# Two transformer blocks on one core: routing rebuilt, level scores in half-width products, and matmuls moved into waits

## The chip, the cores and the metric

The kernel runs on one NeuronCore of a Trainium2 chip. The metric is device time in microseconds, the median of several executions. The engines named here are TensorE (PE, with its weight load PEld), VectorE (DVE), ScalarE (ACT), GpSimd (POOL) and SyncE (SP), whose queue starts most of the DMAs.

## The reference

x is 256 tokens by 1024, f32. Two blocks run one after the other. Shortened to what matters here:

```
# block one
h = rmsnorm(x);  parts = h @ w_in
o_a = gated delta rule(short conv + silu of q, k, v)        # rope positions serve branch b
o_b = attention over 64 keys that an indexer chose (top-k)
x = x + (sigmoid(gate_a)*(o_a @ w_proj_a) + sigmoid(gate_b)*(o_b @ w_proj_b)) @ w_out
# experts: top 1 of 4 groups, then top 2 of the 4 experts in it
gsel = argmax(glog);  top_p, top_i = top_k(softmax(elog[gsel]), 2)
wts = softmax(glog)[gsel] * top_p / sum(top_p)
x = x + sum_e wts_e * (silu(xt @ w1_e) * (xt @ w3_e)) @ w2_e;   x = rmsnorm(x)
# block two
branch a: scores[t,s] = sum_c q[t,c] k[s,c] exp(b[t,c] - b[s,c]), s <= t, then state; branch b: attention
x = x + (gates and branches) @ w_out_2;   x = x + ffn(x);   x = x + sigmoid(.. @ w_ple_gate) * (p @ w_ple_proj)
```

The activations are f32. Weights and activations of the large products are split into a rounded part (fp32r) and the remainder, and each product is three matmuls: high by high, low by high, high by low.

## The kernel before

**Weights.** About 148 chunks of up to 128 x 2048 words come in one fixed order through a ring of four raw buffers (SP, L478). ScalarE rounds a chunk into `w_hi` (`ahead`, L566) and VectorE subtracts it into `w_lo` (`ahead`, L1838); each of these two has three buffers. `ahead(i)` splits all chunks up to i + 2. A raw buffer is loaded again when its low part is made, so the split of one chunk releases the load of the fourth after it. Every engine's program is written out by hand, in one order, with semaphores between them; an engine does not pass a wait, so all that is queued behind it waits too.

**Block one up to its routing.** TensorE makes the convolution's channels, turns them (`turn_y`, L1225) and makes the token blocks in between. ScalarE takes the turned tiles out of PSUM (L700); ahead of that stands the sine for the rope (L692), for which VectorE reduces the angles (down to L1965). Gate chunks 0 to 7 fill TensorE's time beside the delta rule and the top-k; ScalarE takes each out with a sigmoid (`gate_sigmoid`, L686). Chunk 7 goes to bank 7 as one, and the first projection, into banks 6 and 7, waits for both of its sigmoids. Then come `turn_probs` (L1480), `prob_times_v` (L1491) and projections (`project`, L1056 to L1059). `prob_times_v` waits until ScalarE has the turned probabilities in SBUF (L817); its outputs are 64 columns wide in the array, one half for even heads and one for odd. VectorE has the softmax and its multiplication (L2204) in its order between weight splits.

**Routing.** After the last half of x is ready, ScalarE sums squares, TensorE turns x and multiplies by the router (L1522). VectorE picks the group (`one_hot`), with L1879 in the root before it. TensorE sums the ranks of the tokens in their groups (`ranks`, L1555 to L1559, f32), among them the group counts, last. VectorE orders the groups by count (L2389 on), writes `order_i` (L2395), by which SP knows whose expert weights to load, and then the one-hot matrix `place` of token by slot (L2405). `gather` (L1564) multiplies x by `place` in f32 for each of the eight column groups; ScalarE and VectorE split each result (`gathered_high`, `gathered_low`). Between these VectorE works out the expert weights of each token and puts them into `scal` (`s_comb`); `slot_tiles` (L1584, L1589) multiplies them to slots and turns `place`. Expert 0's gate comes as two half chunks (`FIRST`, `FIRST + 1`), then `slot_tiles`, then the up chunk (`FIRST + 2`, L1542 to L1544). All 16 experts follow.

**Level scores of block two.** The scores of branch a are made level by level: for level n a pair of operands is multiplied, 8 tiles of 128 x 128 (L1711), and VectorE takes the masked places into `hsc` (`copy_predicated`, L2483). Level 0 takes the diagonal, levels 1 to 6 places inside the two 64 x 64 diagonal blocks, level 7 the block between the halves. Between levels stands one weight chunk (`LVL2[n]`, L1111 to L1113).

**End of attention in block two.** Gate chunks 6 and 7, `turn_probs`, `prob_times_v`, then projections; ScalarE evicts gate 7 ahead of the turned probabilities. GpSimd multiplies each gate chunk by a row of roots (L546).

## Time and profile before

| | |
|---|---|
| median of 3 runs | 903.81 us (903.46 to 904.65) |
| profiled execution: time / span | 902.36 us / 900.6 us |
| busy: PE, PEld, DVE, ACT, POOL | 97%, 90%, 69%, 54%, 5% of the span |
| mean granted TensorE clock | 0.994 of full |
| DMA | 156.73 MB, mean 174 GB/s |
| TensorE busy in the stretch 260 to 280 us | 14.56 of 20 us |
| TensorE busy in the stretch 500 to 560 us | 60 of 60 us |

A row of the timeline has start, duration, engine, line, operation, tiles and the number of instructions merged, and in brackets how long the engine was idle before it and what ended that. A matmul's duration includes its way through the array, so in a stream the starts, not the durations, tell the rate. One f32 product is two passes, and each stands in the trace as an instruction. `128*64` is 128 rows by 64 columns of the array in use.

### The profile page before, as it was taken

Reading aid. Unit: us, or ns where it says so; the run is one execution under the profiler, and the core shown is the slowest. Engines: PE = TensorE matmul, PEld = TensorE weight load, DVE = VectorE, ACT = ScalarE, POOL = GpSimd, SP = SyncE. Lnnn points to the kernel's source line nnn. Section 1 sums busy time; section 2 is a strip of 40 time slices with the busy share of each in tenths; the row PEclk is TensorE's granted clock in tenths of the full one; section 3 lists DMA queues with packets and bytes.
Section 4 is the critical chain, followed back from the end, with each engine's and each line's share of the span. In section 5 each row is a group of like instructions: output and inputs, shape, how many; then the busy total and the mean of one; then the engine's idle time right before and its main releaser. Section 6 shows DMA issues by size and latency. Waiting matters only on the chain.

```text
span 900.6 us, 16480 instructions
## 1 busy us (share of the span) xinstructions
PE 873.4 (97%) x7186; PEld 809.4 (90%) x7186; DVE 622.4 (69%) x761; ACT 484.6 (54%) x580; POOL 43.2 (5%) x66
## 2 busy tenths in 40 slices
PE   8999999998998999999999999999999999999997
PEld 8988899998977999999979888998989999999986
DVE  6879477698847964568887887886565655555564
ACT  5647713657525754367766643767545443343463
POOL 6000060000000000000000000121000000000000
PEclk9999999999998999999999999999999999999999
DMA  8846310424107985569975444253355656556421
GB/s 248 292 148 212 94 51 3 141 95 141 47 1 252 363 302 206 186 237 360 359 229 192 165 141 140 95 194 128 101 188 176 209 190 199 173 186 199 176 94 47
DMA packets 88904, 156.73 MB, mean 174 GB/s; under 512 B 7432, under 2 KB 61184, under 8 KB 84864
## 3 DMA queue, kind: packets, MB, share of 16 engines
q1 hardware_dynamic: 88144, 154.90, 50.9%
q8 instruction: 56, 0.92, 0.4%
q10 hardware_dynamic: 688, 0.79, 0.3%
q14 instruction: 16, 0.13, 0.0%
HBM read 154.62 MB, written 1.05 MB: 173 GB/s over the span
## 4 chain that ended last, share of the span: by engine, by line
PE 77%; DVE 14%; ACT 4%; SPq 2%; issue 2%; DMA 1%; POOL 0%; DVEq 0%; POOLq 0%; ACTq 0%
PE ps L1056 9%; PE ps L1059 8%; PE ps L1058 8%; PE ps L1111 7%; PE ps L1112 7%; PE ps L1113 7%; DVE w_lo L1838 5%; PE ps L1542 4%; PE ps L1543 4%; PE ps L1544 4%; PE ps L1310 3%; PE ps L1614 2%; PE ps L1616 2%; PE ps L1615 2%; ACT w_hi L566 2%
## 5 line engine op out<-in xcount | busy, mean ns | idle before, releaser
L1838 DVE TENSOR_TENSOR w_lo<-raw,w_hi 128x2048 fp32r<-128x2048 f32 (+2 forms) x148 | 334.1, 2263 | 136.7 <-ACT w_hi L566 135.4
L566 ACT ACTIVATE w_hi<-raw 128x2048 fp32r<-128x2048 f32 (+2 forms) x148 | 277.8, 1881 | 81.4 <-PE ps L1113 27.4
L1056 PE MATMUL ps<-h_hi,w_hi 128*128 128x256 f32 x736 | 210.5, 286 | 2.2 <-DVE h_lo L1848 1.4
L1058 PE MATMUL ps<-h_lo,w_hi 128*128 128x256 f32 x736 | 208.2, 283 | 0.0
L1059 PE MATMUL ps<-h_hi,w_lo 128*128 128x256 f32 x736 | 208.2, 283 | 0.0
L1056 PEld LDWEIGHTS ps<-h_hi,w_hi 128*128 128x128 f32 x736 | 141.1, 192 | 4.8 <-issue 3.2
L1058 PEld LDWEIGHTS ps<-h_lo,w_hi 128*128 128x128 f32 x736 | 141.1, 192 | 0.4
L1059 PEld LDWEIGHTS ps<-h_hi,w_lo 128*128 128x128 f32 x736 | 141.1, 192 | 0.0
L1111 PE MATMUL ps<-w_hi,h_hi 128*128 128x512 f32 (+1 forms) x240 | 93.9, 391 | 0.5 <-DVE h_lo L2247 0.5
L1112 PE MATMUL ps<-w_lo,h_hi 128*128 128x512 f32 (+1 forms) x240 | 92.7, 386 | 0.0
L1113 PE MATMUL ps<-w_hi,h_lo 128*128 128x512 f32 (+1 forms) x240 | 92.6, 386 | 0.0
L1542 PE MATMUL ps<-w_hi,arena_rounded 128*128 128x256 f32 x320 | 91.1, 285 | 0.7 <-DVE w_lo L1838 0.6
L1544 PE MATMUL ps<-w_hi,arena_rounded 128*128 128x256 f32 x320 | 89.4, 280 | 0.0
L1543 PE MATMUL ps<-w_lo,arena_rounded 128*128 128x256 f32 x320 | 89.4, 279 | 0.0
L1542 PEld LDWEIGHTS ps<-w_hi,arena_rounded 128*128 128x128 f32 x320 | 60.0, 188 | 1.9 <-DVE w_lo L1838 1.1
L1543 PEld LDWEIGHTS ps<-w_lo,arena_rounded 128*128 128x128 f32 x320 | 60.2, 188 | 0.5
L1544 PEld LDWEIGHTS ps<-w_hi,arena_rounded 128*128 128x128 f32 x320 | 60.0, 188 | 0.0
L1111 PEld LDWEIGHTS ps<-w_hi,h_hi 128*128 128x128 f32 x240 | 45.1, 188 | 8.7 <-DVE h_lo L2247 0.7
L1113 PEld LDWEIGHTS ps<-w_hi,h_lo 128*128 128x128 f32 x240 | 45.1, 188 | 8.4
L1112 PEld LDWEIGHTS ps<-w_lo,h_hi 128*128 128x128 f32 x240 | 45.2, 188 | 7.9
L1056 PE MATMUL ps<-o_hi,w_hi 128*128 128x256 f32 x128 | 36.6, 286 | 2.0 <-DVE w_lo L1838 1.0
L1111 PE MATMUL ps<-w_hi,o_hi 128*128 128x512 f32 x96 | 37.8, 394 | 0.3 <-DVE o_lo L2285 0.3
(456 smaller groups left out, 1352.1 us busy)
## 6 DMA issues: line engine op xcount, KB each, us to landing
raw<-in_w_in SPq DMA_DIRECT2D x35, 1024.0 KB, 5.3
raw<-in_w_exp_up SPq DMA_DIRECT2D x16, 1024.0 KB, 6.0
raw<-in_w_exp_down SPq DMA_DIRECT2D x16, 1024.0 KB, 5.7
raw<-in_w_exp_gate SPq DMA_DIRECT2D x15, 1024.0 KB, 5.8
raw<-in_w_ffn_gate SPq DMA_DIRECT2D x11, 1024.0 KB, 5.4
raw<-in_w_ffn_up SPq DMA_DIRECT2D x11, 1024.0 KB, 5.4
raw<-in_w_ffn_down SPq DMA_DIRECT2D x11, 1024.0 KB, 4.9
raw<-in_w_out SPq DMA_DIRECT2D x8, 1024.0 KB, 5.1
```

What stands on the lines that cost most here:

```text
L566: act.activation(w_hi[:, j % SPL, 0:kt * n], raw[:, j % RAW, 0:kt * n], ACT.Copy).then_inc(w_high, 1)
L1056: pe.matmul(o, hi[:, k, cols], a_hi[:, k, :], start=(k == 0 and (whole or c == 0)), stop=False)
L1058: pe.matmul(o, hi[:, k, cols], a_lo[:, k, :], start=False, stop=False)
L1059: last_mm = pe.matmul(o, lo[:, k, cols], a_hi[:, k, :], start=False, stop=(k == kt - 1 and (whole or c == len(outs) - 1)))
L1111: pe.matmul(o, a_hi[:, k, tok], hi[:, k, cols], start=(first and k == 0), stop=False)
L1112: pe.matmul(o, a_hi[:, k, tok], lo[:, k, cols], start=False, stop=False)
L1113: last_mm = pe.matmul(o, a_lo[:, k, tok], hi[:, k, cols], start=False, stop=(end and k == kt - 1))
L1310: m = pe.matmul(by_head(o, rows_c, h), left[rows_c, t, h, :], right(rows_c, h), start=True, stop=True)
L1542: pe.matmul(o, xs_hi[:, k, slots], hi[:, w_k, :], start=(k == 0), stop=False)
L1543: pe.matmul(o, xs_hi[:, k, slots], lo[:, w_k, :], start=False, stop=False)
L1544: last_mm = pe.matmul(o, xs_lo[:, k, slots], hi[:, w_k, :], start=False, stop=(k == KD - 1))
L1838: dve.tensor_tensor(w_lo[:, j % SPL, 0:kt * n], raw[:, j % RAW, 0:kt * n], w_hi[:, j % SPL, 0:kt * n].bitcast(F32), sub).then_inc(w_ready, 1)
```

## The change

- `w_in` part: the sine (L692) goes behind the six evictions of turned tiles; the semaphores of positions and p are joined with others.
- The last gate chunk of block one is made tile by tile, the first into bank 7, the second into bank 6, each with its own sigmoid; the first projection begins with the two tiles of bank 7.
- A third tile of projection (0, 1, 0) goes ahead of `prob_times_v`; in block two half of gate chunk 7 goes behind `turn_probs`, and its eviction behind `prob_tiles`.
- Level scores: levels 0 to 6 multiply only the two 64 x 64 diagonal blocks, level 7 only the block between.
- Routing: the choice of group is written in bf16 too, the counts are multiplied first and signalled by themselves, in bf16. Expert choice moves behind the slots, the gathered low parts and the splits of the first three expert chunks, and is worked out by comparisons of all pairs. x is rounded into `x_hi` by ScalarE behind its squares and `x_lo` is subtracted by GpSimd; the gather is four fp32r products for each column group. GpSimd also makes `tok_pos`. TensorE turns the identity 10 times ahead of the ranks and 24 times behind them.

```diff
@@ scalar, block one
-            ahead(TOK[0][0])
-            act.wait_ge(s_trig, 1)
-            act.activation(cs[:, :, :, :], cs[:, :, :, :], ACT.Sin).then_inc(s_sin, 1)
...
                 act.activation(qkv[:, t, 512 * g:512 * g + 512], bank(j % 4), ACT.Copy).then_inc(s_qkv, 1)
+            act.wait_ge(s_trig, 1)
+            act.activation(cs[:, :, :, :], cs[:, :, :, :], ACT.Sin).then_inc(s_sin, 1)
...
-            gate_sigmoid(7)
+            last_gate_sigmoid()
@@ scalar, in front of the routing
                 squares(1, c)
+                cols = slice(512 * c, 512 * c + 512)
+                act.activation(x_hi[:, :, cols], x_tok[:, :, cols], ACT.Copy).then_inc(s_x_hi, 1)
@@ scalar, routing()
-                for k in range(4):
+                for k in range(6):
                     gathered_high(k)
                 ahead(FIRST + 1 - SPL)
-                for k in range(4, 6):
-                    gathered_high(k)
-                ahead(FIRST + 2 - SPL)
@@ gpsimd
+            for c in range(2):
+                pool.wait_ge(s_x_hi, c + 1)
+                cols = slice(512 * c, 512 * c + 512)
+                pool.tensor_tensor(x_lo[:, :, cols], x_tok[:, :, cols], x_hi[:, :, cols].bitcast(F32),
+                                   ALU.subtract).then_inc(s_x_lo, 1)
+            pool.wait_ge(s_place, 1)
+            step(pool.tensor_tensor(ttmp_p, ga1.unsqueeze(2)..., sel16.unsqueeze(1)..., ALU.mult))
+            for j in range(1, 4):
+                step(pool.tensor_tensor(tok_pos, ttmp_p[:, :, :, 0] if j == 1 else tok_pos, ttmp_p[:, :, :, j], ALU.add))
+            pool.tensor_copy(scal[:, :, 16], r_moe).then_inc(s_comb, 1)
@@ tensor, last gate and projections of block one
-            gate_chunk(GATE, 7, s_gate_ev)
+            for c in range(2):                  # tile 0 to bank 7, tile 1 to bank 6 behind gate 6's eviction
+                if c == 1:
+                    pe.wait_ge(s_gate_ev, 7)
...
+                m.then_inc((s_last_gate, w_used)[c], 1)
+            pe.wait_ge(s_last_gate, 2)
+            project(PROJ, 0, 0, 0, (2, 3), False)
             pe.wait_ge(s_gate_ev, 8)
-            project(PROJ, 0, 0, 0)
+            project(PROJ, 0, 0, 0, (0, 1), True)
...
             turn_probs(prob, 0, range(2, 6))
+            project(PROJ, 0, 1, 0, (2,))
             prob_times_v(prob_t, ..., 0)
-            project(PROJ, 0, 1, 0, range(2, 4))
+            project(PROJ, 0, 1, 0, (3,))
@@ tensor, ranks(), gather(k), routing()
+                pe.matmul(bank(3)[:, 8:12], ones_bf[:, :], g[:, 0, :], start=True, stop=False)
+                pe.matmul(bank(3)[:, 8:12], ones_bf[:, :], g[:, 1, :], start=False, stop=True).then_inc(s_small_ps, 1)
+                pe.matmul(o[:, 0:4], upto_bf[:, :], g[:, 0, :], start=True, stop=True)
...
-                for t in range(NT):
-                    m = pe.matmul(bank((4 + k) % 8)[:, 0:S], by_row(x_tok)[:, t, k, :], place[:, t, :],
-                                  start=(t == 0), stop=(t == NT - 1))
+                for part in (x_hi, x_lo):
+                    for t in range(NT):
+                        m = pe.matmul(bank((4 + k) % 8)[:, 0:S], by_row(part)[:, t, k, :], place_r[:, t, :], ...)
...
+                idle_turns(10)
                 ranks()
+                idle_turns(24)
                 pe.wait_ge(s_place, 1)
+                pe.wait_ge(s_x_hi, 2)
+                pe.wait_ge(s_x_lo, 2)
@@ tensor, level scores
+                blocks = ((0, 0), (1, 1)) if n < len(LEVELS) else ((0, 1),)
                 for u in range(8):
                     b = bank(2 * (n % 2) + u // 4)[:, P * (u % 4):P * (u % 4) + P]
                     left, right = (hk[:, u, :], hq[:, u, :]) if n == 0 else (hx[:, n % 2, u, :],) * 2
-                    m = pe.matmul(b, left, right, start=True, stop=True)
+                    for keys, queries in blocks:
+                        r, c = slice(64 * keys, 64 * keys + 64), slice(64 * queries, 64 * queries + 64)
+                        m = pe.matmul(b[r, c], left[:, r], right[:, c], start=True, stop=True)
@@ tensor, block two
-            gate_chunk(GATE2, 7, s_gate_ev2)
+            gate_chunk(GATE2, 7, s_gate_ev2, range(4))
             turn_probs(prob2, 2)
+            gate_chunk(GATE2, 7, s_gate_ev2, range(4, 8))
@@ vector, routing
-            one_hot(ga1, gl, gs1)
-            dve.nop().then_inc(s_group, 1)
+            is_top(ga1, gl, gs1)
+            dve.tensor_tensor(group_bf[:, :, :], ga1, last(gs2, 4), ALU.is_equal).then_inc(s_group, 1)
+            step(dve.tensor_tensor(ga1, ga1, last(gs2, 4), ALU.is_equal))
...
+            step(dve.memset(lower, 0.0))        # with the other constants, ahead of the merge of block one
+            for i in range(1, 4):
+                m = mark(dve.memset(lower[:, i, 0:i], 1.0))
+            dve.wait_ge(s_dve, m)
...
             m.then_inc(s_place, 1)
+            ...                                 # the group's expert logits and both shifts, 5 instructions
+            for k in range(4):
+                gathered_low(k)
+            ahead(FIRST + 1 - SPL)
+            for k in range(4, 8):
+                gathered_low(k)
+            ahead(FIRST + 2 - SPL)
+            ahead(FIRST + 3 - SPL)
             dve.wait_ge(s_rle, 2)
             step(dve.tensor_reduce(gs3, gl, X, add_))
+            step(dve.tensor_tensor(ttmp, by_j, by_i, ALU.is_equal))
+            step(dve.tensor_tensor(ttmp, ttmp, lower..., mult))
+            step(dve.tensor_tensor(above, by_j, by_i, ALU.is_gt))
+            step(dve.tensor_tensor(ttmp, ttmp, above, add_))
+            step(dve.tensor_reduce(e1h, ttmp, X, add_))
+            step(dve.scalar_tensor_tensor(e1h, e1h, 1.5, el, ALU.is_lt, mult))
+            ...                                 # sum, factors, reciprocal: 5 instructions
+            dve.wait_ge(s_comb, 1)
             dve.tensor_tensor(scal[:, :, 0:16]..., last(tok_pos, 4), e1h..., mult).then_inc(s_comb, 1)
```

## Rows read from the trace of the kernel before

**Rows 1.** The page: the chain that ended last, and a group of instructions.

```profile
PE 77%; DVE 14%; ACT 4%; SPq 2%; issue 2%; DMA 1%; POOL 0%; DVEq 0%; POOLq 0%; ACTq 0%
...
L566 ACT ACTIVATE w_hi<-raw 128x2048 fp32r<-128x2048 f32 (+2 forms) x148 | 277.8, 1881 | 81.4 <-PE ps L1113 27.4
```

**Rows 2.** Waits, whole span: total us, times, longest.

```profile
ACT cs L692 <- DVE cs L1965: 4.7, 1, 4.7
...
DVE arena L2483 <- PE ps L1711: 10.1, 7, 2.4
...
PE ps L1491 <- ACT arena L817: 1.9, 2, 1.0
PE ps L1225 <- ACT arena L700: 1.6, 1, 1.6
```

**Rows 3.** Timeline of TensorE, 205 to 216 us: start, duration, instructions.

```profile
207.11 0.39 PE L1056 MATMUL ps<-o_hi,w_hi 128*128 128x256 f32 x1 [0.93 <-ACT arena L686]
...
213.41 1.06 PE L1480 MATMUL ps<-ident,arena 128*128 128x128 f32 x8 [0.28 <-DVE arena L2204]
```

**Rows 4.** Timeline of TensorE around narrow products and one level.

```profile
512.60 1.95 PE L1711 MATMUL ps<-arena 128*128 128x128 f32 x16
514.30 0.48 PE L1111 MATMUL ps<-w_hi,h_hi 128*128 128x512 f32 x1
...
156.38 0.68 PE L1381 MATMUL ps<-arena 64*64 64x64 f32 x16
156.89 1.09 PE L1391 MATMUL ps<-arena 64*64 64x64 f32 x16
...
221.41 3.11 PE L1491 MATMUL ps<-arena 128*64 128x128 f32 x48 [0.84 <-ACT arena L817]
```

**Rows 5.** Timeline of TensorE in the routing.

```profile
269.10 0.59 PE L1555 MATMUL ps<-small,upto 128*128 128x4 f32 x2 [1.59 <-DVEq L2380]
...
274.83 9.36 PE L1564 MATMUL ps<-arena,x_tok 128*128 128x256 f32 x32 [3.43 <-DVE arena L2405]
...
287.43 1.06 PE L1584 MATMUL ps<-small,arena 128*128 128x17 f32 x8
...
289.62 0.39 PE L1542 MATMUL ps<-w_hi,arena_rounded 128*128 128x256 f32 x1 [0.65 <-DVE w_lo L1838]
```

**Rows 6.** Windows: busy of PE, PEld, DVE, ACT, POOL; granted clock; DMA.

```profile
268.00:269.00 1.00, 0.00 (x0) 0.00 (x0) 0.82 (x5) 0.00 (x0) 0.00 (x0) 0.50 0.00 0
277.00:278.00 1.00, 1.00 (x3) 0.73 (x3) 0.45 (x2) 0.44 (x1) 0.00 (x0) 0.50 1.03 381
278.00:279.00 1.00, 1.00 (x6) 1.00 (x5) 0.11 (x2) 0.47 (x1) 0.00 (x0) 0.92 1.00 385
```

**Rows 7.** Timeline of VectorE in the routing.

```profile
266.19 0.17 DVE L1879 TENSOR_SCALAR small<-small 128x2 f32<-128x2 f32 x1
...
271.43 0.16 DVE L2389 SCALAR_TENSOR_TENSOR small<-ps,small 128x4 f32<-128x4 f32 x1 [1.40 <-PE ps L1559]
...
272.67 0.17 DVE L2395 CAST order_i<-small 128x4 int32<-128x4 f32 x1
```

**Rows 8.** DMA issues from 274.8 us: count, KB, median us to landing.

```profile
raw<-in_w_exp_up SPq DMA_DIRECT2D x1, 1024.0 KB, 7.8
```

**Rows 9.** GpSimd's line L546: duration ns min/median/max.

```profile
L546 POOL TENSOR_TENSOR arena<-arena x8: 1270/1864/2119, 576.4 to 625.3; 128x512 f32<-128x512 f32 x8
```

**Rows 10.** Timeline of all engines, 576 to 578.5 us.

```profile
576.36 1.95 POOL L546 TENSOR_TENSOR arena<-arena 128x512 f32<-128x512 f32 x1 [445.21 <-ACT arena L674]
...
577.47 0.87 DVE L2524 TENSOR_SCALAR small<-small 128x16 f32<-128x16 f32 x1
```

**Rows 11.** Timeline of SyncE's queue and of VectorE's split of that chunk.

```profile
274.81 0.37 SPq L478 DMA_DIRECT2D raw<-in_w_exp_up  x1
...
287.28 2.29 DVE L1838 TENSOR_TENSOR w_lo<-raw,w_hi 128x2048 fp32r<-128x2048 f32 x1
```

More of the change, by code:

```diff
@@ L262, in two_block_program @@
         act_s2, act_p2 = (view(4096 + 1024 * n, 2, NT, D_EXP) for n in range(2))
-        place = view(6144, NT, S)
+        place_r = view(6144, NT, S, of=arena_rounded)
+        place = place_r.bitcast(F32)
+        x_hi, x_lo = (view(12288 + 2048 * n, NT, DM, of=arena_rounded) for n in range(2))
         x_cols = view(18448, KD, S)
@@ L322, in two_block_program @@
         top8b = small[:, 464:472]
+        lower = split3(small[:, 536:552], 4)
+        above, ttmp_p = (split4(small[:, first:first + 32], 2, 4) for first in (552, 584))
         glog_twice = split3(small[:, 536:616], 2)
@@ L2363, in _, with is_top @@
             root_of(1, r_moe)
-            def one_hot(dst, src, top):
+            def is_top(dst, src, top):
                 step(dve.tensor_reduce(top, src, X, ALU.max))
@@ L2370, in one_hot @@
                 step(dve.tensor_reduce(gs2, dst, X, ALU.max))
-                step(dve.tensor_tensor(dst, dst, last(gs2, 4), ALU.is_equal))
             dve.wait_ge(s_small_ps, 1)
@@ L2404, in _ @@
             for t in range(NT):
-                m = dve.tensor_scalar(place[:, t, :], count, slot2[:, t:t + 1], None, ALU.is_equal)
+                m = dve.tensor_scalar(place_r[:, t, :], count, slot2[:, t:t + 1], None, ALU.is_equal)
             m.then_inc(s_place, 1)
+            step(dve.tensor_tensor(ttmp, rl[:, :, 4:20].rearrange("p t (g j) -> p t g j", j=4), last(ga1, 4), mult))
+            step(dve.tensor_reduce(el, ttmp.rearrange("p t g j -> p t j g"), X, add_))
+            dve.tensor_tensor(gl, gl, last(gs1, 4), sub).then_inc(s_rlm, 1)
@@ L2408, in _ @@
+            step(dve.tensor_reduce(gs3, el, X, ALU.max))
+            dve.tensor_tensor(el, el, last(gs3, 4), sub).then_inc(s_rlm, 1)
+            for k in range(4):
[5 more added lines that the diff above has]
+            ahead(FIRST + 3 - SPL)
             dve.wait_ge(s_rle, 2)
             step(dve.tensor_reduce(gs3, gl, X, add_))
-            step(dve.reciprocal(gs3, gs3))
```

95 lines of the change are left out of this document (47 added, 48 removed).

## The prediction

> **What bounds the kernel now.** I read the page's chain first: 77% of it is TensorE's own work and 14% VectorE's [rows 1]. So a microsecond is won only where TensorE works less, or where it stands waiting. The list of waits then shows where it stands: 1.6 us at the turn of the convolution tiles (L1225), 1.9 us in two waits ahead of probabilities times values (L1491), and the routing [rows 2, 5]. There TensorE starts the ranks at 269.10, the gather at 274.83, the slot tiles at 287.43 and the first up chunk at 289.62. The windows show its clock at 0.50 from 268 on, and back during 278 to 279: it fell after small router matmuls and half a microsecond of waiting, and rose 3.4 us into the gather [rows 6]. The level stage of the second block has no TensorE wait; VectorE waits for it 10.1 us in 7 times [rows 2]. All times are those of the profiled execution.
>
> **The change part by part.**
>
> *Sine behind the evictions.* ScalarE stood 4.7 us in front of the sine (L692), and everything behind it was late, up to the eviction that TensorE waited 1.6 us for at L1225 [rows 2]. With the sine moved behind the six evictions that wait goes: TensorE reaches the turn 1.6 us earlier, ScalarE is by then through. The sine's result is wanted far later. **-1.6 us** (bounds 0 and -1.7).
>
> *Last gate chunk in two tiles.* It removes the 0.93 us before L1056 at 207.11. But the next thing TensorE needs is the probabilities: it waits for VectorE's L2204 at 213.41, and VectorE has come there from the top-k without a pause [rows 3]. The stall only moves there: **0** (bounds 0 and -0.9).
>
> *Project tile ahead of probabilities times values; last half gate chunk likewise in block two.* Each fills a wait of about 0.95 us at L1491 [rows 2] with 12 or 24 matmuls that stood behind it. In the first block VectorE's path to the merge starts earlier by it, but gets four memsets with two semaphore waits in front of it, about 0.2 us. **-0.7 and -1.0 us** (bounds 0 and -1.9 together). The later eviction of gate 7 in block two stays covered: its sigmoid comes after the projections.
>
> *The level scores.* Today 8 levels have 16 passes of 128x128 each, started at 512.60, and the next weights follow at 514.30: 1.70 us a level [rows 4]. After, seven levels have 32 passes of 128 rows by 64 columns, with 64 moving columns, alternating between the two column halves; the eighth has 16, all in one half. No row has this form. The nearest: L1381 alternates between column halves in the same 64 rows and takes 156.89 - 156.38 = 0.51 us for 16 passes, 32 ns each; L1491 alternates over all 128 rows with 128 moving columns, 48 passes in 3.1 us, 64 ns each, where a full-width pass of the same length takes 106 ns. So halves do run side by side. L1391, all in one corner, starts 16 passes within 1.09 us less the 0.22 us of its last: 58 ns each [rows 4]. At 29 to 32 ns a level costs 0.93 to 1.0 us, and the eighth 16 x 0.058 = 0.93. Entering and leaving the narrow form costs about 0.1 us each: L1491 ends 3.11 us after its start, though 48 x 0.055 would be 2.6. I take 1.13 us a level, so 8 x (1.70 - 1.13) = **-4.6 us**; without the switches -6.2, with 0.3 us of them -3.8; and, if halves took turns, 7 x (1.86 + 0.2 - 1.70) - 0.6 = +1.9. VectorE has 10.1 / 7 = 1.4 us to spare in a level [rows 2], so it does not become the bound at 0.6 us less.
>
> The Trainium skill (TensorEngine Tiling (Array Packing), Key Properties) says that a change of tiling mode drains the engine, here twice a level. It gives no price; taken as nothing the levels give -6.2 us, with the row's 0.2 us -4.6.
>
> *Routing, the head.* Group counts come first, in bf16. VectorE stood 1.40 us before L2389 at 271.43, for ranks that began at 269.10 at half clock [rows 5, 7]. Two short products in place of ten passes should let it begin 1.75 us earlier. Against that, the low part of x is now subtracted by GpSimd. Its 512 elements take at least 1.27 us [rows 9], so 1024 take 2.5, from about 266.25 (behind the last squares) to 268.8. In the trace L2524, 16 elements, takes 0.87 us and ends at 578.34, when GpSimd's instruction begun at 576.36 ends, at 578.31 [rows 10]; L1879, 2 elements, takes 0.17 [rows 7]. So VectorE's small operations are held by one of GpSimd. The group choice would be held about 0.5 us. I take the order of groups 1.3 us earlier (bounds 0.2 and 1.75), so ready at 272.84 - 1.3 = 271.5, and with it the expert weights' issue.
>
> *Routing, the tail.* Here the expert choice stands behind three chunk splits on VectorE, and the third chunk (first up) has to land. It was issued at 274.81 [rows 11] and landed 7.8 us later, at 282.6 [rows 8], so 9.8 us after the order at 272.84 [rows 7]. The sum after: 271.5 + 9.8 = 281.3 landed; ScalarE's half of the split 1.9 [rows 1] and VectorE's 2.2 [rows 11] with two handovers of 0.1 gives 285.6; then 13 small operations, at the 0.207 us that the six from 271.43 to 272.67 took each, 2.7, gives 288.3; TensorE's slot tiles begin at 288.4 instead of 287.43. They take 1.5 us (289.62 - 287.43 less the 0.65 of waiting), and the up chunk begins at 289.9 against 289.62: **+0.3 us** (bounds -0.2 and +2.5). The gather itself, 9.36 us now [rows 5], is in one pass per product and wholly hidden in this, as long as it ends some 3 us before 281; if it did not, its lateness would be added.
>
> *The clock in the tail.* From the end of the new gather (about 277.5) to 288.4 TensorE has two short half chunks of gate, 1.4 us each, and waits in between, the last one from 283.9 on, 4.5 us; no identity turns are put there. Before, the clock fell after less waiting than that [rows 6]. If it falls, slot tiles and the first up matmuls run at half rate. Before, it rose 3.4 us after steady work began; between once and twice that at half rate costs 1.7 to 3.4 us; I take **+2.4**. Before, this stretch ran at full rate, the low stretch lay under the waits and the gather. What the turns of the identity in the head win, an earlier rise, is spent under the wait for the up chunk.
>
> Sum of the likeliest: -1.6 - 0.7 - 1.0 - 4.6 + 0.3 + 2.4 = -5.2 us, on the profiled execution 902.36 - 5.2 = 897.2. The median of the runs is 1.45 above the profiled one: 903.81 - 5.2 = **898.6**.
>
> **The rivals.**
> - *The clock holds in the tail* (or its loss lies under waits). For: two bursts of work stand in it. Against: 4.5 us of waiting at its end. -7.6 us: 896.2.
> - *GpSimd's subtraction holds VectorE.* It begins within 0.1 us of L1879 at 266.19 [rows 7], a small operation in front of the root. If L1879 comes second it waits until 268.8 and all of the head with it; the order then comes 2 us later than taken. -3.2 us: 900.6. The Trainium skill (SBUF — State Buffer, Who interferes with whom) has this as a lock: a VectorE instruction with two SBUF inputs, or in a two-port mode, and a GpSimd instruction that reads SBUF exclude each other for the whole instruction, and whoever starts first has it; L2524 agrees.
> - *The column halves take turns* (slower side). If a pass with all 128 rows occupied goes one after the other at 58 ns, the levels cost +1.9 instead of -4.6. Against: L1491 and L1381. It decides from about 54 ns a pass on, where seven levels no longer win. The rest is -0.6, so +1.3 us: 905.1.
> - *The filled waits come back.* The wins of L1225 and L1491 are taken by VectorE chains behind them as that of the last gate is. -2.0 us: 901.8.
>
> **How the numbers follow.** Chances: forecast 0.50, clock holds 0.20, GpSimd 0.12, halves take turns 0.10, waits come back 0.08. A measurement of this kernel tells 0.2% (1.8 us) from no change. Faster by more: the first three whole and half of the last, 0.86; within: 0.06; slower by more: 0.08, of the case of turns with its upper bounds. Low end: switches at nothing and the clock holding, -10, 894. High end: GpSimd's hold with a low clock's upper bound, 902.5; nearly all of the turns case is left out.
>
> **What would show it.** L1711 at 29 to 32 ns a pass and 1.1 us a level, VectorE's wait there down from 1.4 to about 0.8 us; no wait at L1225; at L1491 under 0.2 us. The order of groups 1.3 us earlier against the squares, and still the first up chunk not earlier, with TensorE waiting some 4 us before the slot tiles for VectorE's expert choice; the granted clock at 0.50 there. The prediction is wrong if the up chunk lands or the choice is through much sooner, if L1711 passes take over 50 ns, or if the clock stays full.

## The result and the profile after

The changed kernel took 899.1 us (median of 5 runs, 897.85 to 900.15) against 903.81: a ratio of 0.9947, 95% interval 0.9932 to 0.9961. The forecast was 898.6. The profiled execution took 898.25 us, its span 896.5, with a mean granted clock of 0.993; 897.2 was forecast for it.

I set the start of each TensorE instruction beside the start of the same one before. "Shift" below is start after less start before, and the times in the table are those of the kernel before. The difference of two shifts is what the stretch between them won (negative) or lost.

| stretch (shift at its end) | forecast | between the traces |
|---|---|---|
| sine (-1.53 at 128 us) | -1.6 | -1.5 |
| last gate chunk and project tile, block one (-2.13 at 239 us) | 0, -0.7 | -0.6 |
| routing up to the first up matmul (+0.90) | +0.3 | +3.0 |
| low clock behind it (+2.37 at 292 us) | +2.4 | +1.5 |
| experts (+1.01 at 454 us) | 0 | -1.4 |
| eight level scores (-2.95 at 558 us) | -4.6 | -4.0 |
| last half gate chunk, block two (-4.05 at 628 us) | -1.0 | -1.1 |
| sum | -5.2 | -4.1 |

The total came out close to the forecast partly by luck. The routing cost 2.7 us more than forecast and the level scores won 0.6 less; the experts won 1.4 us that was not forecast, and the low clock cost 0.9 less than taken. What is left between the two traces is 1.1 us.

The page of the kernel after, the chain that ended last (to [rows 1]):

```profile
PE 84%; DVE 9%; ACT 2%; SPq 2%; issue 1%; DMA 1%; POOL 0%; DVEq 0%; POOLq 0%
```

TensorE's own work is 84% of the chain now (77% before) and VectorE's 9% (14%).

The waits of the kernel after, whole span (to [rows 2]):

```profile
PE ps L1636 <- DVE small L2490: 3.4, 1, 3.4
...
DVE arena L2537 <- PE ps L1766: 3.2, 3, 1.9
...
PE ps L1521 <- DVE arena L2259: 1.4, 1, 1.4
```

The waits at the turn of the convolution tiles and ahead of probabilities times values are gone. New is the first row: TensorE stands 3.4 us before the slot tiles for the last product of the expert choice. VectorE's waits for the level scores fell from 10.1 us in seven to 3.2 in three. Not all of that is gone: between 500 and 560 us VectorE now waits 2.9 us for ScalarE's rounded chunks (0.9 before). The last row is the wait that the last gate chunk was forecast to hand on: 0.28 us before [rows 3], 1.44 now.

Timeline of TensorE around one level (to [rows 4]):

```profile
519.67 0.39 PE L1142 MATMUL ps<-w_hi,h_lo 128*128 128x512 f32 x1
519.99 1.15 PE L1766 MATMUL ps<-arena 128*64 128x64 f32 x32
521.07 0.50 PE L1140 MATMUL ps<-w_hi,h_hi 128*128 128x512 f32 x1
```

From the first pass to the next weights it is 1.08 us instead of 1.70, with 29 ns from pass to pass on the average (two passes start 7 ns apart, and 58 ns lie between one pair and the next). But the first pass starts 0.32 us behind the last weight pass, and in the kernel before it was 0.23: the period of a level went from 7.24 to 6.75 us, 0.49 less and not 0.57.

Timeline of the routing, of all engines (to [rows 5, 7, 11]):

```profile
264.03 2.34 POOL L555 TENSOR_TENSOR arena_rounded<-x_tok,arena_rounded 128x1024 fp32r<-128x1024 f32 x1 [3.94 <-ACT arena_rounded L953]
264.05 2.35 DVE L1935 TENSOR_SCALAR small<-small 128x2 f32<-128x2 f32 x1
...
270.49 0.17 DVE L2449 CAST order_i<-small 128x4 int32<-128x4 f32 x1
...
272.64 7.98 PE L1612 MATMUL ps<-arena_rounded 128*128 128x256 f32 x32
...
279.12 1.05 ACT L589 ACTIVATE w_hi<-raw 128x1024 fp32r<-128x1024 f32 x1
...
282.91 3.42 DVE L1894 TENSOR_TENSOR w_lo<-raw,w_hi 128x1024 fp32r<-128x1024 f32 x2
...
286.24 0.15 DVE L2476 TENSOR_REDUCE small<-small 128x2 f32<-128x8 f32 x1
...
289.22 1.07 PE L1636 MATMUL ps<-small,arena_rounded 128*128 128x17 f32 x8 [3.37 <-DVE small L2490]
...
290.52 0.36 PE L1584 MATMUL ps<-w_hi,arena_rounded 128*128 128x256 f32 x1
```

Three things are to be seen. VectorE's tensor_scalar of two elements takes 2.35 us beside GpSimd's subtraction, and both end together. The gather takes 8 us. And the choice (L2476 on) begins when VectorE has split the up chunk, which began late: the first expert chunk landed at 275.69, and ScalarE came to it at 279.12, behind six gathered parts.

Windows of the kernel after (to [rows 6]); the third number from the end is the granted clock:

```profile
263.00:264.00 1.00, 0.59 (x4) 0.60 (x4) 1.00 (x3) 0.95 (x2) 0.00 (x0) 0.78 0.00 0
264.00:265.00 1.00, 1.00 (x6) 1.00 (x7) 0.96 (x2) 0.00 (x0) 0.97 (x1) 0.50 0.00 0
...
270.00:271.00 1.00, 1.00 (x9) 1.00 (x8) 0.83 (x7) 0.00 (x0) 0.00 (x0) 0.81 0.00 0
...
290.00:291.00 1.00, 1.00 (x10) 1.00 (x10) 0.65 (x2) 0.14 (x1) 0.00 (x0) 0.93 1.00 418
291.00:292.00 1.00, 1.00 (x7) 1.00 (x6) 1.00 (x1) 0.98 (x2) 0.00 (x0) 0.50 0.18 74
```

The clock falls in the router now, behind a wait of 0.42 us, some 4 us earlier than before, and again behind the slot tiles. That second low stretch was forecast, the first was not.

### The profile page after: what moved, and what is told of

The parts are those of the page before. It is cut to its first block, busy times and chain, and to the rows that moved or that the text cites. A ratio compares the mean times of both kernels' runs of the same rounds, so it can differ in the third digit from the quotient of the medians.

```text
span 896.5 us, 16763 instructions
## 1 busy us (share of the span) xinstructions
PE 873.4 (97%) x7327; PEld 808.8 (90%) x7327; DVE 623.3 (70%) x755; ACT 486.5 (54%) x582; POOL 51.6 (6%) x75
## 3 DMA queue, kind: packets, MB, share of 16 engines
HBM read 154.62 MB, written 1.05 MB: 174 GB/s over the span
## 4 chain that ended last, share of the span: by engine, by line
PE 84%; DVE 9%; ACT 2%; SPq 2%; issue 1%; DMA 1%; POOL 0%; DVEq 0%; POOLq 0%
PE ps L1085 10%; PE ps L1087 10%; PE ps L1088 10%; PE ps L1140 8%; PE ps L1141 8%; PE ps L1142 8%; PE ps L1584 4%; PE ps L1586 4%; PE ps L1585 4%; DVE w_lo L1894 3%; PE ps L1339 3%; PE ps L1666 2%; PE ps L1668 2%; PE ps L1667 2%; ACT w_hi L589 1%
## 5 line engine op out<-in xcount | busy, mean ns | idle before, releaser
L1085 PE MATMUL ps<-h_hi,w_hi 128*128 128x256 f32 x720 | 206.2, 286 | 2.7 <-DVE h_lo L1904 1.4
L1087 PE MATMUL ps<-h_lo,w_hi 128*128 128x256 f32 x720 | 203.8, 283 | 0.0
L1088 PE MATMUL ps<-h_hi,w_lo 128*128 128x256 f32 x720 | 203.8, 283 | 0.0
L1085 PEld LDWEIGHTS ps<-h_hi,w_hi 128*128 128x128 f32 x720 | 138.1, 192 | 5.3 <-issue 3.2
L1087 PEld LDWEIGHTS ps<-h_lo,w_hi 128*128 128x128 f32 x720 | 138.2, 192 | 0.3
L1088 PEld LDWEIGHTS ps<-h_hi,w_lo 128*128 128x128 f32 x720 | 138.1, 192 | 0.0
L1584 PEld LDWEIGHTS ps<-w_hi,arena_rounded 128*128 128x128 f32 x320 | 61.0, 191 | 2.8 <-DVE w_lo L1894 2.3
L1586 PEld LDWEIGHTS ps<-w_hi,arena_rounded 128*128 128x128 f32 x320 | 60.9, 190 | 0.0
```

The costliest lines, as they stand in the source:

```text
L1085: pe.matmul(o, hi[:, k, cols], a_hi[:, k, :], start=(k == 0 and (whole or c == 0)), stop=False)
L1087: pe.matmul(o, hi[:, k, cols], a_lo[:, k, :], start=False, stop=False)
L1088: last_mm = pe.matmul(o, lo[:, k, cols], a_hi[:, k, :], start=False, stop=(k == kt - 1 and (whole or c == len(outs) - 1)))
L1584: pe.matmul(o, xs_hi[:, k, slots], hi[:, w_k, :], start=(k == 0), stop=False)
L1586: last_mm = pe.matmul(o, xs_lo[:, k, slots], hi[:, w_k, :], start=False, stop=(k == KD - 1))
```

## The experiments

Ratios are to the kernel before, measured on the same chip; the changed kernel stands at 0.9947. Times in the expectations that are not of a row are of the kernel named there. Each interval is about 0.0015 to either side, so the difference of two ratios is uncertain by some 0.002, or 1.9 us. Differences below that (e2, e3, e4, e9 and e10 against the changed kernel, e5 against e1) are not shown by the medians alone; where the text says more of them, it rests on the traces.

| run | ratio | 95% interval |
|---|---|---|
| e1 choice first | 0.9907 | 0.9891 to 0.9922 |
| e2 low part on VectorE | 0.9958 | 0.9944 to 0.9972 |
| e3 turns in the tail | 0.9935 | 0.9922 to 0.9949 |
| e4 routing as before | 0.9930 | 0.9916 to 0.9944 |
| e5 choice and order | 0.9892 | 0.9875 to 0.9908 |
| e6 together | 0.9861 | 0.9844 to 0.9877 |
| e7 levels grouped | 1.0019 | 1.0009 to 1.0030 |
| e8 sine only | 0.9985 | 0.9974 to 0.9997 |
| e9 no turns | 0.9957 | 0.9939 to 0.9975 |
| e10 last gate as before | 0.9946 | 0.9929 to 0.9963 |
| e11 fills as before | 0.9984 | 0.9975 to 0.9994 |
| e12 levels only | 0.9955 | 0.9938 to 0.9972 |

### e1: the expert choice ahead of the gathered parts

```diff
+            dve.wait_ge(s_rle, 2)               # the whole choice, up to scal
+            ...
             for k in range(4):
                 gathered_low(k)
             ahead(FIRST + 1 - SPL)
             for k in range(4, 8):
                 gathered_low(k)
             ahead(FIRST + 2 - SPL)
             ahead(FIRST + 3 - SPL)
-            dve.wait_ge(s_rle, 2)
-            ...
```

> The changed kernel with the expert choice (13 small VectorE operations) moved ahead of the gathered low parts and of the splits of the first three expert chunks. Theory A, the choice stands behind the split of the up chunk and only that makes the slot tiles late: the slot tiles begin about 285.7 us instead of 289.22, right behind the second half gate chunk, the first up matmul at about 287.1 instead of 290.52, and as TensorE no longer stands 3.6 us in one piece the clock stays full and the 1.5 us lost between 290.5 and 292 go too: 4.9 us less than the changed kernel, about 894.2. Rival B, the landing of the up chunk and its split bound the up matmuls anyway, so that the slot tiles come earlier but the first up matmul stays at 290 or later: at most 1.5 us less, about 897.6. Rival C, the gathered low parts come later by the 2.7 us of the choice and hold up the first half gate chunk (281.47 in the changed kernel) and all behind it: no gain.

Measured 894.61 us; by the ratios (0.9907 against 0.9947) 3.6 us less than the changed kernel; 4.9 were expected. Its timeline:

```profile
272.53 0.16 DVE L2469 TENSOR_REDUCE small<-small 128x2 f32<-128x8 f32 x1 [0.28 <-ACT small L898]
...
275.16 1.65 DVE L2359 SCALAR_TENSOR_TENSOR arena_rounded<-ps,gain_p,arena_rounded 128x256 fp32r<-128x256 f32 x4
...
284.63 0.96 PE L1636 MATMUL ps<-small,arena_rounded 128*128 128x17 f32 x8
...
285.83 0.36 PE L1584 MATMUL ps<-w_hi,arena_rounded 128*128 128x256 f32 x1
```

The choice now lies in VectorE's idle time at the start of the gather; the first four gathered parts come together behind it. Slot tiles follow the half gate chunk without a wait, and the granted clock is 1.00 from 290 to 291. Theory A holds in its mechanism: the place of the choice cost the changed kernel 3.6 us, wait and clock together. This execution also had the full clock in the router, so its trace alone would say more (shift +2.37 against -2.90 in the expert stage).

### e2: the second half of the low part of x on VectorE

```diff
-            for c in range(2):                  # pool: both halves
+            pool.wait_ge(s_x_hi, 1)             # pool: the first half only
...
             dve.tensor_copy(order_i[:, :], order_f).then_inc(s_order, 1)
+            dve.wait_ge(s_x_hi, 2)
+            dve.tensor_tensor(x_lo[:, :, 512:1024], x_tok[...], x_hi[...].bitcast(F32), sub).then_inc(s_x_lo, 1)
```

> The changed kernel with the second half of the low part of x subtracted by VectorE, behind the writing of order_i, instead of by GpSimd. Theory A, the GpSimd instruction of 2.34 us holds VectorE's tensor_scalar in the root for 2.35 us (both end at 266.4): without it that instruction takes about 0.17 us, the order of groups and with it the issue of the expert chunks come 2 us earlier (1.2 us earlier than that for the gather, since VectorE's own subtraction of about 1.2 us stands ahead of place), and the slot tiles and the first up matmul follow by 2 us: about 897.1. Rival B, the wait of VectorE has another cause (the accumulator of ScalarE's squares coming late): the instruction still takes over 2 us and the time grows by VectorE's 1.2 us or stays, 899 to 900. Rival C, the order comes 2 us earlier but the up matmuls do not, since the split and the choice bind: no change over 0.3 us.

No gain: 0.9958. Yet the hold is as supposed:

```profile
263.96 0.17 DVE L1933 TENSOR_SCALAR small<-small 128x2 f32<-128x2 f32 x1
264.40 0.17 DVE L1935 RECIPROCAL small<-small 128x2 f32<-128x2 f32 x1 [0.27 <-ACT small L953]
266.68 0.38 DVE L2431 SCALAR_TENSOR_TENSOR small<-ps,small,rep 128x20 f32<-128x20 f32 x2 [2.12 <-PE ps L1562]
```

The window of its router; the third number from the end is the granted clock:

```profile
265.00:266.00 1.00, 1.00 (x7) 1.00 (x6) 0.00 (x0) 0.66 (x1) 0.00 (x0) 0.50 0.00 0
```

Without GpSimd beside it the operation takes 0.17 us instead of 2.35. But VectorE then waits 2.12 us for the router, whose 16 passes run at half clock here too; the order came only 0.33 us earlier. The hold and the slow router lie beside each other, so that taking one away wins next to nothing. My 2 us missed that. What it says of rival C is not tested, since the order hardly moved.

The Trainium skill (SBUF — State Buffer, Who interferes with whom) counts tensor_scalar among the operations that can enter a two-port mode and so exclude GpSimd for a whole instruction. The trace agrees: 2.35 us beside GpSimd, 0.17 alone.

### e3: turns of the identity ahead of the slot tiles

```diff
+                        for _ in range(30):
+                            pe.transpose(bank(1)[:, 0:P], ident[:, :], ident[:, :])
                         slot_tiles()
```

> The changed kernel with 30 more turns of the identity on TensorE between the second half gate chunk and the slot tiles, 3.3 us at full clock, where it now stands idle for 3.6 us. Nothing else is moved. Theory A, the clock falls to 0.50 at 291 us because TensorE stood idle ahead of the slot tiles: the granted clock stays at 1.00 through 285 to 296 us, the slot tiles begin at 289.2 as before, and the first up chunk takes 2.8 us instead of 4.3: 1.5 us less, about 897.6. Rival B, the clock falls for the earlier waits between 280 and 284 us: the low stretch stays and nothing is won, 899.1. Rival C, the turns run into the slot tiles or disturb VectorE's choice: the slot tiles are later and the kernel slower by up to 0.5 us.

Measured 897.32 us, 0.9935, about 1.1 us less; the intervals overlap, so its size is uncertain. The windows:

```profile
290.00:291.00 1.00, 1.00 (x12) 1.00 (x11) 0.24 (x2) 0.00 (x0) 0.00 (x0) 1.00 1.03 434
291.00:292.00 1.00, 1.00 (x11) 1.00 (x10) 1.00 (x1) 0.72 (x2) 0.00 (x0) 1.00 0.46 188
```

The clock holds here, so the wait in front of the slot tiles was what let it fall. The other traces agree: the six rebuilt kernels that stand 2.8 to 3.4 us before the slot tiles (changed, e2, e7, e9, e10, e11) are all at half clock there or just behind, and the three without that wait (e1, e5, e6) are not. The expectation was full clock from 285 us on; it did not foresee half clock from 281.7 to 285.1, beginning in the wait of 0.85 us for the first half gate chunk, which this execution shows and the changed kernel's does not. And the shift still grows, from +1.30 to +2.19, behind the first up chunk: TensorE, being faster, waits 0.84 us at 297 us for the second expert's gate chunk. A low clock costs only what the next wait does not take up.

### e4: everything but the routing

```diff
@@ kernel before: sine, last gate, project tile, level scores, half gate chunk as changed
@@ ranks(), gather(k), expert choice, x_hi and x_lo, turns of the identity: not changed
```

> The kernel before with every edit except those of the routing: sine, last gate chunk, project tile, last half gate chunk of block two, level scores. Theory A, by the shifts between the two traces the routing as rebuilt costs 4.3 us from 259 to 294 us (the first up chunk 0.9 us later than before although the routing began 2 us earlier, and 1.5 us more at half clock), so without it the kernel takes 1.4 + 0.6 + 3.95 + 0.6 = 6.6 us less than before: about 897.3, or 1.8 us less than the changed kernel if the 1.8 us that the expert stage has won by its slightly shorter spacing (116.8 instead of 117.8 ns a pass) belong to the rebuilt routing, and 895.4 if that spacing is had without it too. Rival B, the rebuilt routing is worth something that later stages give back only there: 899 or more.

Measured 896.4 us, 0.9930: by the medians the rebuilt routing makes the kernel slower by about 1.5 us, with overlapping intervals; the spans of the profiled executions are 896.5 and 894.6 us. Here too the clock fell in the router, so that the old routing ended at a shift of -0.85 where -2.2 went in. Against that the rebuilt one is 3.2 us later at 292 us (+2.37), and gets 1.4 back from the experts' pace. Theory A holds in its first form: the pace is had only in kernels with the rebuilt routing.

### e5: and the splits between the gathered parts

```diff
-                for k in range(6):              # ScalarE; VectorE in the same order
+                for k in range(4):
                     gathered_high(k)
                 ahead(FIRST + 1 - SPL)
+                for k in range(4, 6):
+                    gathered_high(k)
+                ahead(FIRST + 2 - SPL)
```

> The kernel of e1 (expert choice ahead of the gathered low parts), and on ScalarE and VectorE the splits of the first three expert chunks between the gathered parts again, as in the kernel before: the first behind four, the second behind six, the third behind eight. In e1 the chunks had landed at 274.4, 275.7 and 278.1 us but ScalarE began the first split at 278.04, behind six gathered parts, and TensorE waited 0.85 and 1.03 us for the two low parts. Theory A, the order of the splits holds the first up matmul at 285.83: the first split begins about 1.4 us earlier, the two waits of TensorE shrink or go, and the first up matmul begins 1 to 1.9 us earlier: about 893.2. Rival B, the pace of the gather (0.97 us a column group) and ScalarE's and VectorE's work together bind, so that what the first split wins the last gathered parts lose: within 0.5 us of e1's 894.6.

Measured 893.14 us, 0.9892, 1.4 us under e1's ratio, the intervals overlapping. The waits of 0.85 and 1.03 us ahead of the two half gate chunks are gone; from the gather's start to the first up matmul it is 12.66 us instead of e1's 14.33:

```profile
272.40 7.96 PE L1615 MATMUL ps<-arena_rounded 128*128 128x256 f32 x32
...
283.00 0.96 PE L1639 MATMUL ps<-small,arena_rounded 128*128 128x17 f32 x8
...
285.06 0.38 PE L1587 MATMUL ps<-w_hi,arena_rounded 128*128 128x256 f32 x1 [0.61 <-DVE w_lo L1897]
```

### e6: all of it together

```diff
@@ against the kernel of e5
             root_of(1, r_moe)
+            dve.wait_ge(s_x_hi, 2)              # x_lo's second half here, not on GpSimd
+            dve.tensor_tensor(x_lo[:, :, 512:1024], ...)
...
                 turn_half(1, 1)
+                idle_turns(3)
                 router(range(4, 8))
```

> The kernel of e5, and the second half of the low part of x subtracted by VectorE between the root and the router's result (where it stood idle for 2.1 us in e2), and three turns of the identity ahead of the second half of the router on TensorE. Theory A, with the clock at 1.00 in the router its result comes at 265.2 us, and the order of groups at 268.7, 0.7 us earlier than in e1, because VectorE's 1.2 us of subtraction take the place of the 2.35 us that GpSimd held it for; the gather and all behind it follow by 0.7 us: about 892.5. Rival B, three turns do not keep the clock: the router's passes run at half rate in some executions, the result comes at 266.7 and the order as in e5 or later: 893 to 894.5. Rival C, the subtraction on VectorE delays the router's result by more than it wins: slower than e5.

Measured 891.06 us, 0.9861, 1.4% under the kernel before and the fastest. That is 2.1 us under e5, where 0.7 was expected, while the two profiled executions differ by 0.4 us: the mean clocks of e6's four executions are 0.996 to 0.999, those of e5's 0.993 to 0.995. The subtraction fits into the time in which VectorE waited for the router:

```profile
264.29 1.96 PE L1565 MATMUL ps<-rt_raw,arena 128*128 128x20 f32 x16
...
264.93 0.17 DVE L1937 TENSOR_SCALAR small<-small 128x2 f32<-128x2 f32 x1
...
265.57 1.22 DVE L2426 TENSOR_TENSOR arena_rounded<-x_tok,arena_rounded 128x1024 fp32r<-128x1024 f32 x1
```

The router's 16 passes start within 1.7 us, at full clock; in the changed kernel it was 3.1. That the three turns did it is not shown: in e1's and e11's profiled executions the clock held there without them.

The traces together say what each of the two costs in the head. From the first of the router's last 16 passes to the end of the writing of `order_i`:

| | clock full in the router | clock falls in the router |
|---|---|---|
| routing as before | 7.3 us (before, e12) | 8.6 (e4) |
| rebuilt, GpSimd holds VectorE | 6.6 (e1, e11) | 7.25 (changed) |
| rebuilt, no hold | 5.6 (e6) | 7.0 (e2) |

So the hold costs 1.05 us while the router is fast and 0.2 while it is slow, and the slow router costs 0.6 beside the hold and 1.45 without it. Each cell is one or two executions; with the hold and a fall that came later in the router (e3, e5, e7, e9, e10; 1.9 to 2.9 us for the passes) it is 6.6 to 6.9.

### e7: level scores half by half

```diff
-                for u in range(8):
-                    for keys, queries in blocks:
+                for keys, queries in blocks:
+                    for u in range(8):
                         pe.matmul(b[r, c], left[:, r], right[:, c], start=True, stop=True)
```

> The changed kernel with the 16 passes of a level score (levels 0 to 6) in another order: first the eight 64-column blocks of the lower half, then the eight of the upper, instead of the two halves in turn. Same work, same number of passes. Theory A, a pass of 128 rows by 64 columns takes 58 ns by itself and two run side by side only where they follow each other in different column halves: a level's scores take 0.9 us longer or nearly that (16 passes at about 60 ns a pass of 29 to 32 before), 7 levels 3 to 6 us: 902 to 905 us. Rival B, the halves do not run side by side and the saving is from 64 columns instead of 128 alone: no change, 899.

Measured 905.29 us, 1.0019. A level's row:

```profile
522.81 1.90 PE L1766 MATMUL ps<-arena 128*64 128x64 f32 x32
```

It is 58 ns from pass to pass instead of 29, and a period of 7.50 us against 6.75. So the saving hangs on the order alone: in turn, two passes run side by side; half by half, they follow one another, and that is dearer than the full-width passes. By the ratios the kernel is 6.5 us slower than the changed one, and 3 to 6 were expected: the levels make 5.3 of it between the traces, and the rest was lost before them (shift +2.34 against +1.01 at 454 us). The Trainium skill (TensorEngine Tiling (Array Packing), Key Properties) says that different tiles can load and multiply in parallel; 29 against 58 ns agrees.

### e8: the sine alone

```diff
@@ kernel before, ScalarE
-            act.wait_ge(s_trig, 1)
-            act.activation(cs[:, :, :, :], cs[:, :, :, :], ACT.Sin).then_inc(s_sin, 1)
...
                 act.activation(qkv[:, t, 512 * g:512 * g + 512], bank(j % 4), ACT.Copy).then_inc(s_qkv, 1)
+            act.wait_ge(s_trig, 1)
+            act.activation(cs[:, :, :, :], cs[:, :, :, :], ACT.Sin).then_inc(s_sin, 1)
```

> The kernel before with the sine moved behind the six evictions and nothing else. Theory A: the wait of TensorE at the turn of the convolution tiles (1.6 us) goes and nothing takes it back: 1.5 us less, 0.9983 of before. Rival B: the chain of VectorE behind the delta rule takes it back by the last gate chunks at 207 us: no change.

Measured 901.82 us, 0.9985: 1.4 us less (0.3 to 2.4), as Theory A has it. The shift stands at -2.12 us at 128 us in its profiled execution, so the wait is gone. But in that execution something does take it back: the shift is still -2.05 at 262 us, but -0.77 behind the gather and -0.53 at 454 us. The clock fell in the router here, and the gather began 1.8 us earlier but came back to full clock 5.7 us after its start, at 278.7, where it was 3.4 us before. What a win ahead of the routing is worth thus also depends on the clock in it.

### e9: no turns around the ranks

```diff
-                idle_turns(10)
                 ranks()
-                idle_turns(24)
```

> The changed kernel without the 34 turns of the identity around the ranks. Theory A, the turns are worth nothing in the time: the clock then rises inside the gather instead of ahead of it, the gather ends 0.5 to 2 us later, but the wait for the expert choice (3.4 us ahead of the slot tiles) takes that up only if the splits on ScalarE do not come later; since those stand behind six gathered parts, I expect them and the first up matmul to be later by what the gather is: 1 to 2 us more, 900 to 901. Rival B, without the 10 turns the ranks start 0.3 us earlier at VectorE's group choice and the gather's pace, which is set by its weight loads, is little slower at half clock: no change, 899. The spacing of the experts' passes: 116.8 ns if the expert stage's faster pace does not hang on the number of TensorE's instructions ahead of it, 117.8 if it does.

Measured 899.85 us, 0.9957, no difference from 0.9947. The gather, and the clock in it:

```profile
273.16 7.98 PE L1612 MATMUL ps<-arena_rounded 128*128 128x256 f32 x32 [3.42 <-DVE arena_rounded L2458]
```
```profile
275.00:276.00 1.00, 1.00 (x6) 1.00 (x5) 0.49 (x2) 0.48 (x2) 0.00 (x0) 0.50 1.06 410
276.00:277.00 1.00, 1.00 (x6) 1.00 (x6) 0.53 (x2) 0.48 (x1) 0.00 (x0) 0.50 1.07 434
```

The gather takes 7.98 us, its first 5.4 at half clock (until 278.6 us), and it takes 7.98 at full clock in the changed kernel: rival B. What the turns buy is worth nothing there. The experts' spacing stays at 116.8 ns, so it does not hang on these 34 instructions.

### e10: the last gate chunk as before

```diff
@@ changed kernel
-            for c in range(2): ...              # two tiles, two banks, two sigmoids
-            project(PROJ, 0, 0, 0, (2, 3), False)
-            project(PROJ, 0, 0, 0, (0, 1), True)
+            gate_chunk(GATE, 7, s_gate_ev)
+            pe.wait_ge(s_gate_ev, 8)
+            project(PROJ, 0, 0, 0)
```

> The changed kernel with the last gate chunk of block one and the first projection as before. Theory A, the split of the last gate only moves TensorE's wait of 0.93 us from the projection to the turned probabilities: the wait of 0.9 us at the first projection comes back, that ahead of the turned probabilities falls from 1.44 to about 0.5, and the time is that of the changed kernel within 0.2 us. Rival B, it is worth its 0.9 us: 900.

Measured 898.61 us, 0.9946; the shift at 239 us is -2.11 against -2.13. The wait goes back to where it was:

```profile
205.63 0.39 PE L1085 MATMUL ps<-o_hi,w_hi 128*128 128x256 f32 x1 [0.93 <-ACT arena L709]
...
211.90 0.84 PE L1509 MATMUL ps<-ident,arena 128*128 128x128 f32 x6 [0.25 <-DVE arena L2247]
```

### e11: the filled waits as before

```diff
@@ changed kernel
-            project(PROJ, 0, 1, 0, (2,))
             prob_times_v(prob_t, ..., 0)
-            project(PROJ, 0, 1, 0, (3,))
+            project(PROJ, 0, 1, 0, range(2, 4))
...
-            gate_chunk(GATE2, 7, s_gate_ev2, range(4))
+            gate_chunk(GATE2, 7, s_gate_ev2)
             turn_probs(prob2, 2)
-            gate_chunk(GATE2, 7, s_gate_ev2, range(4, 8))
```

> The changed kernel with the third project tile of block one and the last half gate chunk of block two behind probabilities times values again. Theory A: the two waits there come back, 0.85 us in block one and 1.0 us in block two, and the kernel takes 1.6 us more, 900.7. Rival B, in block one the shift of 0.6 us between the traces is less than the wait because the chain on VectorE behind it has slack of its own: 0.3 to 1 us more.

Its waits, whole span:

```profile
PE ps L1532 <- ACT arena L847: 1.9, 2, 1.0
```

The two waits are back with 1.9 us, and 902.15 us (0.9984) is 3.3 us more than the changed kernel, twice what was expected. In its profiled execution the clock also fell between 210 and 220 us, which it did in e3, e6 and e9 too but not in the changed kernel's; this and the routing explain the rest of that trace (shift -0.18 at 239 us instead of -2.13). Whether the added wait makes that fall likelier stays open.

### e12: the level scores alone

```diff
@@ kernel before
-                    m = pe.matmul(b, left, right, start=True, stop=True)
+                    for keys, queries in blocks:
+                        m = pe.matmul(b[r, c], left[:, r], right[:, c], start=True, stop=True)
```

> The kernel before with the level scores in half-width products and nothing else. Theory A, nothing else of the change touches this stage, so each of the 8 levels is 0.49 us shorter as between the two traces: 3.9 us less, 0.9957 of before. Rival B, a part of it is given back later in the block, by VectorE's chain: under 3 us.

Measured 899.13 us, 0.9955. The shift goes from 0 to -3.43 us at 558 us with the eighth level's weights. Theory A holds. By the ratios this one edit gives 4.1 us of the whole change's 4.8: most of what the other edits win (3.2 us between the traces) the routing takes back.

## Why the prediction was right, and where not

The total was right, and most of the change's gain (the level scores, the sine, the filled waits) came by the mechanisms named. The routing did not go as told.

- **Sine: right.** -1.5 between the traces, -1.4 alone (e8).
- **Last gate chunk at nothing: right**, and by the mechanism named: VectorE's chain to L2204 ends last there (e10).
- **Filled waits: right,** -0.6 and -1.1 for -0.7 and -1.0.
- **Level scores: right in mechanism, 0.6 us too high in size.** Passes take 29 ns and alternate halves (e7). The mis-sized term is "entering and leaving the narrow form costs about 0.1 us each". Together they are 0.28 us a level: 1.70 less 32 passes at 29 ns would be 0.77 saved, and the period fell by 0.49. About 0.13 lies at the entry (0.09 ahead of the first pass, 0.04 between the first pair and the second) and 0.12 to 0.14 at the exit. The forecast also had VectorE's wait for the scores at 0.8 us a level; it is 3.2 us in all, and 2.0 us more stand before ScalarE's chunks. The Trainium skill (TensorEngine Tiling (Array Packing), Key Properties) has the drain without a price; the trace agrees and prices it.
- **Routing, the head: failed.** "I take the order of groups 1.3 us earlier": against the landmark at 239 us it was 0.05 earlier. Two terms were wrong. GpSimd's hold was costed at 0.5 us; the instruction was held for 2.2, which moves the order by 1.05 at full clock (e1 and e11 against e6). And the clock in the router was put at nothing: it fell there, and the last 16 passes took 3.1 us from first to last start instead of 1.7. The rival with the hold met the right instruction, but e2 shows that the router would have kept the order late without it. The fall is not the rebuilt routing's doing, since the old one has it too in e4. Counted from the router, the rebuilt head writes the order 1.4 us sooner than the old one where the clock falls in both (changed against e4), and 0.7 where it falls in neither (e1 and e11 against before).
- **Routing, the tail: failed by 2.5 us.** The step said that "the gather itself ... is in one pass per product and wholly hidden in this". It ends at 280.6 us. A pass takes 240 ns, as each f32 pass did before at full clock (9.36 us for 32, [rows 5], its first 3.4 us at half clock), so that halving the passes of a product and doubling the products left 32 passes and 8 us. ScalarE's splits stood behind six of its parts. I had let the split of the up chunk begin when it landed; from landing to the end of its low part it took 6.8 us and not 4.3. The landing itself came 8.8 us behind the order, 1 us sooner than taken. The choice took 2.9 us (2.7 were forecast) in the place forecast for it, and moving it wins 3.6 us (e1).
- **Clock in the tail: right in mechanism, +1.5 for +2.4.** It fell behind the wait named (e3). The size is of one execution: half clock lasted from 290.9 to 294.3 us here and in e2 about as long, but from 288.7 at the earliest to 296.1 at the latest, 6.8 us each, in e7, e9, e10 and e11.
- **Not foreseen: the experts' pace.** From 300 to 450 us a pass of 128x256 takes 117.8 ns in the four kernels with the old routing (before, e4, e8, e12) and 116.8 in all ten with the rebuilt one. (The kernel before has a short stretch from 315 to 325 us at 114 to 115.) It gives back 1.4 us. The experts' code is the same; neither turns (e3, e9) nor the order of the head (e6) move it. One difference was not looked at: the ten kernels declare three new tiles (`upto_bf`, `ones_bf`, `group_bf`) ahead of others, among them the one that holds the experts' tokens, so that those may lie at other addresses. No run changes that alone, and the cause stays open.
- **Sums.** Four numbers of the prediction do not follow from its own terms. Seven levels stop winning from about 47 ns a pass on, not 54, if the two changes of form cost 0.2 us. The filled waits coming back give -1.9 us, 901.9, not -2.0. The low end, switches at nothing and the clock holding, is -9.2, 894.6, not -10; the high end as described is 901.6, not 902.5. None of them decides anything here.

The +2.7 us forecast for the routing was +4.5 up to 292 us and +3.1 with the experts. Against e4, in which the clock fell in the router too, the rebuilt routing costs 1.9 us in the spans. So the forecast's +2.7 was met within half a microsecond only with the experts' gain, which it did not know of.

## What to carry to other kernels

Before an operation is moved "behind" others on an engine, list when each of those can begin, not when its data lands: here eight parts of a gather paced both engines. A choice that fits into idle time at the start of a stage should stand there. When two things hold a chain side by side, one engine locked and another slow, costing either alone gives a win that is not there. And an edit whose stage the clock disturbs is to be compared with a kernel in which the clock did the same.

Narrow products like these (128 rows by 64 columns, 64 moving) pay in two column halves when they alternate, and going into the narrow form and out again costs 0.28 us.

## What the hardware showed that was not expected

- The gather's passes: 240 ns with rounded operands at either clock level; f32 passes 239 ns at 2.4 GHz and 427 at 1.2. The experts' passes of the same 128x256 take 117. The stationary operand of the gather is every eighth word of x, that of the experts is contiguous. The Trainium skill (SBUF — State Buffer, Door 1: The DMA port swizzle) says that accesses which cross to a new 16-byte line pay a penalty; a weight load that pays it at every word would fit, but no run here changes the stride alone.
- The clock's falls differ between executions of one program: the changed kernel's five had mean clocks of 0.988 to 0.997 and times of 900.15 to 897.85 us. In the router, with the same wait of 0.42 us ahead of it, the last 16 passes started within 1.70 us in four of thirteen profiled executions (before, e1, e11, e12), within 1.8 to 1.9 in two, and took 2.4 to 3.1 us in seven; e6, whose three turns left a wait of 0.09 us, took 1.70. So a profile of one execution tells the mechanism of such a fall, and only the median what it costs.
